# The delta-rule recurrence of a two-block network in 8 steps of 64 tokens, with one merge of the inverse from 32x32 tiles, in place of 4 chunks of 128

## The reference

```python
def step(S, inp):
    r_t, w_t, k_t, v_t, a_t, b_t = inp
    sa = jnp.einsum('bhvk,bhk->bhv', S, a_t)
    S = (S * w_t[:, :, None, :] + sa[..., None] * b_t[:, :, None, :]
         + v_t[..., None] * k_t[:, :, None, :])
    return S, jnp.einsum('bhvk,bhk->bhv', S, r_t)
...
o_rwkv = rwkv7_time_mix(rw, shift_mu, w0, w2, a0, a2, k_k, k_a, r_k,
                        ln_w, ln_b) * jax.nn.silu(rw_g)
branches = jnp.stack([o_pool, o_ret, o_rwkv], axis=2)
```

## Time and profile before

| | us |
|---|---|
| median of 3 runs | 1938.61 (1937.83 to 1939.07) |
| the profiled execution | 1933.25 |
| its span | 1931.4 |

### The profile page before, as it was taken

One profiled execution on the slowest core, in us unless ns is written; L12 is line 12 of the kernel. 1 busy time (PEld: TensorE's weight loads), 2 busy tenths in 40 slices (PEclk: granted clock), 3 DMA queues, 4 the chain that ended last, 5 costly groups with the idle time before them and its releaser, 6 DMA issues. The chain is left out here.

```text
span 1931.4 us, 24518 instructions
## 1 busy us (share of the span) xinstructions
PE 1814.2 (94%) x9920; PEld 1465.0 (76%) x9920; DVE 1107.9 (57%) x1423; ACT 775.6 (40%) x1148; POOL 645.7 (33%) x374
## 2 busy tenths in 40 slices
PE   8999999999999999899999999998999999988883
PEld 6877799888888877688988888886888987544441
DVE  5255856556777333676554766754215635967675
ACT  3346211233222344531123332234336744866673
POOL 1338411334444433661224344443441021222220
PEclk7999999999999999999999999998999999999997
DMA  8232300214555233331012355433531027999994
GB/s 330 88 110 86 100 22 1 77 56 141 186 174 185 89 120 91 105 88 56 1 55 77 120 186 176 155 121 120 167 103 43 1 90 287 378 388 395 391 395 178
DMA packets 78152, 286.44 MB, mean 148 GB/s; under 512 B 26281, under 2 KB 26409, under 8 KB 60756
## 3 DMA queue, kind: packets, MB, share of 16 engines
q1 hardware_dynamic: 72260, 274.42, 40.6%
q0 software_dynamic: 5040, 8.25, 1.3%
q10 hardware_dynamic: 736, 2.14, 0.3%
...
## 5 line engine op out<-in xcount | busy, mean ns | idle before, releaser
L1523 POOL TENSOR_TENSOR wmem_r<-wmem,wmem_r 128x1024 fp32r<-128x1024 f32 x170 | 419.2, 2467 | 652.3 <-ACT wmem_r L1035 641.3
L705 PE MATMUL banks<-h_hi_r,wmem_r 128*128 128x512 f32 x1632 | 510.4, 391 | 10.2 <-POOL wmem_r L1523 10.1
L705 PEld LDWEIGHTS banks<-h_hi_r,wmem_r 128*128 128x128 f32 x1632 | 307.0, 188 | 80.3 <-POOL wmem_r L1523 13.4
L1035 ACT ACTIVATE wmem_r<-wmem 128x1024 fp32r<-128x1024 f32 x170 | 180.1, 1060 | 438.4 <-DMA wmem<-wstream 435.2
L705 PE MATMUL banks<-hT_r,wmem_r 128*128 128x512 f32 x816 | 318.1, 390 | 0.0
L705 PEld LDWEIGHTS banks<-hT_r,wmem_r 128*128 128x128 f32 x816 | 153.6, 188 | 31.3
L2724 DVE TENSOR_TENSOR slots_r<-slots,wmem_r 128x1024 fp32r<-128x1024 f32 x102 | 122.0, 1219 | 56.2 <-ACT wmem_r L2417 50.7
L2805 POOL TENSOR_TENSOR wmem_r<-wmem,wmem_r 128x1024 fp32r<-128x1024 f32 x30 | 74.8, 2495 | 203.0 <-ACT wmem_r L2275 203.0
L1463 DVE SCALAR_TENSOR_TENSOR ztp<-xT,c_act,ztp 128x256 f32<-128x256 f32 x168 | 129.6, 771 | 6.0
L986 PE MATMUL banks<-slots_r,wmem_r 128*128 128x512 f32 x512 | 127.7, 389 | 0.0
L725 PE MATMUL banks<-wmem_r,h_hi_r 128*128 128x512 f32 x384 | 121.6, 398 | 0.0
...
...
## 6 DMA issues: line engine op xcount, KB each, us to landing
...
```

Source lines behind the costliest of these rows:

```text
L705: mm = nc.tensor.matmul(o, r(lhs[:, k, :]), r(rhs[:, k, :]), start=(k == 0 and i == 0), stop=(k == KD - 1 and i == 2))
L1035: inc(nc.scalar.activation(r(chunk(b)[0]), w, ACT.Copy), "w_high")
L1523: inc(g.tensor_tensor(r(lo), lo, r(hi), ALU.subtract), "w_split")
```

## The change

The recurrence goes in 8 steps of 64 tokens. The inverse needs one level, from 32x32 to 64x64, and that is made for all steps together before the first (`corner_products`: `zp`, then `zc`), with 32x32 matmuls. For it, the DMAs bring the inverted tiles straight into `zt`, and their transposes (a VectorE copy `inv_turned`, stored and spread too) into `tt`; ScalarE copies the off-diagonal tiles from the dg banks into the corner of `zt`.

In a step m, one half of the partitions holds the values v of its 64 tokens, the other the corrections u (`v_side`, `u_side`; they swap with m). K and b are stacked in the same way, so that one matmul over 128 rows takes both: w, s and y are each 8 matmuls of 128x64 by 64. GpSimd copies the v of even steps into `uv_even`. The state has 64 columns per pair of heads, and products with it, grams and dg take the two heads in turn, on partitions 0 to 63 and 64 to 127. The grams of step m+3 stand between w and u of step m. Masks are per step parity (`even`, `odd`) and cover keys and values at once. The LoRA products z and a alternate. GpSimd's pooling buffers move from `ztp` to `xT`.

```diff
-OFF = -DECAY * P / 2
+STEP = P // 2
+STEPS = T // STEP
+OFF = -DECAY * STEP / 2
...
+    in_step, to = row % STEP, np.arange(STEP)[None, :]
+    for name, value_rows in (("even", row < STEP), ("odd", row >= STEP)):
+        put(name, np.concatenate([in_step <= to, (in_step < to) & value_rows], 1))
...
+        uv_even = [rstd[:, :], u_sb]
+        memory = state[:, :, :].rearrange("p c f -> p (c f)")[:, 0:CW * RW_D].rearrange("p (c f) -> p c f", c=CW)
+        side_of = [slice(0, STEP), slice(STEP, P)]
+        v_side = lambda m: side_of[m % 2]
+        u_side = lambda m: side_of[(m + 1) % 2]
+        sub_of = lambda m, q: slice(u_side(m).start + q * SUB, u_side(m).start + (q + 1) * SUB)
+        uv_of = lambda m: v_tok[:, m // 2, :] if m % 2 else uv_even[m // 2 % 2]
+        bk_of = lambda m: (bk_odd if m % 2 else bk_even)[:, m // 2, :]
+        per_head = lambda a: a.rearrange("p (c e f) -> p e c f", c=CW, e=2)
...
+        GRAMS_FIRST = 3
+        for m in range(GRAMS_FIRST):
+            gram_jobs(m)
+        for name, ready in (("zp", "p_ready"), ("zc", "z_ready")):
+            for x in range(NT // 2):
+                for e in range(2):
+                    job(f"{name}{x}{e}", ready, 1 + 2 * x + e)
+        for m in range(STEPS):
+            for e in range(2):
+                job(f"w{m}{e}", "w_ready", 1 + 2 * m + e)
+            if m + GRAMS_FIRST < STEPS:
+                gram_jobs(m + GRAMS_FIRST)
+            for e in range(2):
+                job(f"u{m}{e}", "u_ready", 1 + 2 * m + e)
+            if m < STEPS - 1:
+                job(f"s{m}", "s_added", 1 + m)
+            for e in range(2):
+                job(f"y{m}{e}", "y_ready", 1 + 2 * m + e)
...
+            inc(sp.dma_start(by_row(turned_dram), inv_tmp), "inv_stored", 16)
+            after("z_clear", 1)
+            after("inv_stored", 32)
             for k in range(SUBS):
-                inc(sp.dma_start(inv_part[sub_rows(k)].rearrange("i n h j -> i (n h) j"),
-                                 inv_dram[k].rearrange("n h i j -> i (n h) j")), "inv_spread", 16)
+                q = k % 2
+                inc(sp.dma_start(zt[sub_rows(k), :, q * SUB:(q + 1) * SUB], by_sub(inv_dram, k)), "inv_spread", 16)
+                if q == 0:
+                    inc(sp.dma_start(tt[sub_rows(k), :, :], by_sub(turned_dram, k)), "inv_spread", 16)
...
-            for name, p0 in (("z", 0), ("a", 64)):
-                for c in range(CW):
+            for c in range(CW):
+                for name, p0 in (("z", 0), ("a", 64)):
...
+            for x in range(NT // 2):
+                o = [open_bank(f"dg{x}{e}") for e in range(2)]
+                for i in range(2 * CW):
+                    n, c = 2 * x + i // CW, i % CW
+                    for m in (2 * n, 2 * n + 1):
+                        for e in range(2):
+                            half = side_of[e]
+                            mm = nc.tensor.matmul(o[e][u_side(m), i * STEP:i * STEP + STEP], A_[half, c, m * STEP:m * STEP + STEP],
+                                                  KK[half, c, m * STEP:m * STEP + STEP], start=True, stop=True)
+                            if i == 2 * CW - 1 and m % 2 == 1:
+                                full(mm)
...
-                transposes(f"tb{n}", [A_[:, c, n * P:n * P + P] for c in range(CW)])
+                o = open_bank(f"tb{n}")
+                for c in range(CW):
+                    for m in (2 * n, 2 * n + 1):
+                        mm = nc.tensor.matmul(o[u_side(m), c * P:c * P + P], A_[:, c, m * STEP:m * STEP + STEP], ident, start=True, stop=True)
+                full(mm)
...
+            def gram(m):
+
+                o, t0 = [open_bank(f"gram{m}{e}") for e in range(2)], m * STEP
+                for c in range(CW):
+                    for e in range(2):
+                        half = side_of[e]
+                        for lhs, rows in ((K_, v_side(m)), (A_, u_side(m))):
+                            mm = nc.tensor.matmul(o[e][rows, c * P:c * P + P].rearrange("p (k t) -> p k t", k=2), lhs[half, c, t0:t0 + STEP],
+                                                  slots[half, 0::8, c, t0:t0 + STEP], start=True, stop=True)
+                        if c == CW - 1:
+                            full(mm)
...
+            def corner_products(name, lhs, rhs, to):
+
+                for x in range(NT // 2):
+                    if name == "zc":
+                        after("p_ready", 2 * x + 2)
+                    o = [open_bank(f"{name}{x}{e}") for e in range(2)]
+                    for i in range(2 * RW_H):
+                        for e in range(2):
+                            at = sub_of(e, 1 - to)
+                            mm = nc.tensor.matmul(o[e][sub_of(e, to), i * SUB:i * SUB + SUB], lhs(at, 2 * RW_H * x + i), rhs(at, 2 * RW_H * x + i),
+                                                  start=True, stop=True)
+                            if i == 2 * RW_H - 1:
+                                full(mm)
+
+            for m in range(GRAMS_FIRST):
+                gram(m)
+            after("inv_spread")
+            after("corner_ready")
+            corner_products("zp", lambda at, i: zt[at, i, SUB:STEP], lambda at, i: tt[at, i, :], 1)
+            corner_products("zc", lambda at, i: tt[at, i, :], lambda at, i: zt[at, i, SUB:STEP], 0)
+            after("tok_ready")
+            heads = [slice(c * RW_D, c * RW_D + RW_D) for c in range(CW)]
...
+            def state_part(o, z, m, rows, first, last):
+
+                for c in range(CW):
+                    for e in range(2):
+                        half = side_of[e]
+                        mm = nc.tensor.matmul(o[e][rows, heads[c]], z[half, c, m * STEP:m * STEP + STEP], memory[half, c, :],
+                                              start=(first and c == 0), stop=(last and c == CW - 1), skip_group_check=True)
...
+            for m in range(STEPS):
+                uv, bk = per_head(uv_of(m)), per_head(bk_of(m))
+
+                after("gram_ready", 2 * m + 2)
+                if m % 2 == 0:
+                    after("v_copied", m // 2 + 1)
+                o_w = [open_bank(f"w{m}{e}") for e in range(2)]
+                for e in range(2):
+                    for c in range(CW):
+                        mm = nc.tensor.matmul(o_w[e][u_side(m), heads[c]], gm[:, m % 4, e, c, 1, :], uv[:, e, c, :],
+                                              start=(c == 0), stop=(m == 0 and c == CW - 1), skip_group_check=True)
+                    if m == 0:
+                        full(mm)
+                if m > 0:
+                    after("s_ready", m)
+                    state_part(o_w, KK, m, u_side(m), False, True)
+                if m + GRAMS_FIRST < STEPS:
+                    gram(m + GRAMS_FIRST)
+
+                for e in range(2):
+                    o_u = open_bank(f"u{m}{e}")
+                    after("w_ready", 2 * m + e + 1)
+                    after("z_ready", 2 * (m // 4) + 2)
+                    for c in range(CW):
+                        mm = nc.tensor.matmul(o_u[u_side(m), heads[c]], zt[u_side(m), RW_H * (m // 2) + 2 * c + e, :],
+                                              w_sb[u_side(m), e * CW * RW_D + c * RW_D:e * CW * RW_D + (c + 1) * RW_D], start=True, stop=True)
                     full(mm)
-                for g in range(2):
...
+
+                if m < STEPS - 1:
+                    o_s = open_bank(f"s{m}")
+                o_y = [open_bank(f"y{m}{e}") for e in range(2)]
+                if m > 0:
+                    state_part(o_y, R_, m, v_side(m), True, False)
+                after("u_ready", 2 * m + 2)
+                if m < STEPS - 1:
                     for c in range(CW):
-                        nc.tensor.matmul(o[:, c * P:c * P + P], z[:, c, t0:t0 + P], state[:, c, :],
...
+                        for e in range(2):
+                            mm = nc.tensor.matmul(o_s[side_of[e], heads[c]], bk[:, e, c, :], uv[:, e, c, :], start=True, stop=True)
                     full(mm)
-                if n == 0:
...
+                for e in range(2):
                     for c in range(CW):
-                        cols = slice(c * P, c * P + P)
...
+                        mm = nc.tensor.matmul(o_y[e][v_side(m), heads[c]], gm[:, m % 4, e, c, 0, :], uv[:, e, c, :],
+                                              start=(m == 0 and c == 0), stop=(c == CW - 1), skip_group_check=True)
                     full(mm)
...
+            for m in range(STEPS):
+                for e in range(2):
+                    inc(nc.scalar.activation(w_sb[u_side(m), e * CW * RW_D:(e + 1) * CW * RW_D], bank(f"w{m}{e}")[u_side(m), 0:CW * RW_D], ACT.Copy), "w_ready")
+                if m % 2 == 1 and m // 2 < RING:
+                    high(FIRST["retq"] + m // 2)
+                for e in range(2):
+                    o = bank(f"y{m}{e}")[v_side(m), 0:CW * RW_D].rearrange("p (c f) -> p c f", c=CW)
```

(26 more changed lines are left out.)

319 lines of the change are left out of this document (81 added, 238 removed).

## The result

The median is 1837.47 us (four runs, 1833.72 to 1840.28) against 1938.84 for the kernel before on the same chip: a ratio of 0.9489, with an interval of 0.9476 to 0.9503, or 101 us less. The rival that says that row groups overlap (1856) was nearest.

The account below looks back on a forecast made before the run. TensorE's own work was taken to bound the recurrence. Per layer -21.4 + 1.4 + 5.4 - 1.5 - 1.9 - 1.4 = -19.4 us, -38.8 in both, from the median 1938.61: 1900 us, range 1850 to 1942.

Parts of the forecast that it names:

- The unit of 62 ns: Recurrence: each recorded fp32 matmul pass in the change's new forms costs 62 ns; 1232 passes make 76.4 us per layer.
- rival 1: Recurrence: row groups overlap, 848 alternating passes at 40 ns; -41.2 us per layer, 1856 us; chance 0.25.
- rival 2: w, y and s: full-height passes stay at 112 ns; -1.0 us per layer, 1937 us, no change; chance 0.08.
- Diagonal and turned products: Ahead of the recurrence, per layer: diagonal products 7.9 us, +1.4; turned corrections 7.2 for 1.8 us, +5.4.
- LoRA: LoRA products: z and a alternate between row groups and overlap throughout, 3.4 us and the tail; -1.5 us per layer.
- clock behind the stage: Behind the recurrence: full clock instead of half at the projection; -1.4 us per layer.
- GpSimd: TensorE's 1.95 us wait before 202.72 goes, as TensorE gets there some 5 us later; -1.9 us per layer.
- Changes of form: Recurrence steps: two changes per step between 64- and 128-row forms, 0.1 us each, 1.6 us.
- Waits in the steps: Steps 5 to 7: without a gram between w and u, u waits 0.7 us each, 2.1 us.
- way back: Recurrence steps: u1's copy (428 ns) ends under y-state products (1.0 us); 1.1 us behind s lie under y and next w.
- The inverse: Before the merges: in place near 246, TensorE comes for it at 248, so it costs nothing.
- Rival 3: Merges and steps: clock falls; whole stage at half is +49.6 us per layer, 2038 us; chance 0.12.

Follow-up runs that it names:

- a4: Kernel before with only order changed: a pair's two heads alternate in its grams, z and a in the LoRA products; 1930.08 us, ratio 0.9977.
- a3: Kernel after with the same instructions reordered so that neither row groups nor column sides alternate within a run; 1866.40 us, ratio 0.9651.

## Why the prediction was wrong

**The unit of 62 ns: the step that failed.** I took L874 (one quarter, 64 weight columns, 62 to 68 ns) and L1974 (alternating row groups, 63 ns), saw the same number, and read it as a floor on every pass. The two rows differ in two things: L1974 loads 128 weight columns. a4 shows what its alternation brings: L819's form goes from 75 to 56 ns when the groups alternate (5.03 and 3.84 us, less a tail of 0.3, over 63). So 63 was the overlapped price of a dear form, and 62 the lone price of a cheap one, and there was no floor. The right comparison was L1974 with L819, one form in two orders, 63 ns against 77; L792, which alternates at 71, made it look like little.

And the trace of before did hold the form that I said no row shows, 128 rows with 64 weight columns, and two column sides in turn, in the last block (its 16 matmuls write the two sides alternately):

```profile
1625.92 1.14 PE L2176 MATMUL banks<-ztp 128*64 128x47 f32 x32
1626.99 1.22 PE L2168 MATMUL banks<-ztp,hT 128*128 128x64 f32 x9
```

That is 33 ns a pass, what s takes in the kernel after. So "none of its short runs is faster than about 62 ns" was false, and this one row would have refuted the floor before any run.

The Trainium skill (TensorE: Matmul & The Clock Gate, Part 1, "Wait — 56ns, not 53.3ns?") states the floor that made me sure, about 62 ns per matmul where the sequencer's software decodes it; here 64 matmuls, 128 passes, take 2.10 us, 33 ns each, so that floor doesn't bind in this kernel.

**The sum.** The recurrence was forecast at 81.1 us and is 60.7 and 56.4. By the runs, the error of 62 us splits into 28 for what a lone pass costs (a3: 67 gained where 39 were forecast) and 31 for the overlap; the 3 left are within the intervals. The traces place the parts: a3's two stages take 142.8 us where 162.2 were forecast and the kernel after needs 117.0, and most of the rest of both lies in the diagonal and turned products ahead of them. The sum by rival 1 (1856, 40 ns for what alternates) had half of the mechanism: it used 40 ns where 15 to 33 were measured, and left the column sides out. That it came within 19 us is in part luck, as it also lacks the late inverse and the half clock.

**Full height.** Right: w and y take 58 to 64 ns with 64 weight columns where 128 took 112; rival 2 fell.

**Diagonal and turned products.** From the bonus products on, L810 took 2.1 us (7.9 forecast) and L821 3.9 for 64 passes (7.2). But TensorE then waits 1.34 us for ScalarE's copies of the blocks, for banks: from L810 to the rg projection it is 12.1 us, 11.8 before. The +6.8 became +0.3.

**LoRA, clock behind the stage, GpSimd.** The first two right: 1.8 us less for the LoRA products and 1.4 less from their start to the bonus products (1.5 forecast); the retention projection starts at full clock, and the stretch behind it, up to the merge of the branches, is 1.6 us shorter (1.4 forecast). The wait for GpSimd's chunk did not go: 1.95 us before, 0.8 after in layer 0, since TensorE gets there 1 us later and not 5; over the execution these waits fell from 10.1 to 6.9 us.

**Changes of form.** Right, 0.1 us each: y goes on to the next w, of the same form, after 0.93 us, and w to the state products, of another, after 1.03.

**Waits in the steps.** Right in place: w's copy in steps 5 to 7 (0.5 us each, 0.7 forecast). Not foreseen: u's copy holds s for 0.2 to 0.6 us in each step, as the y-state products over it, priced at 1.0 us, take about half. The way back that was "covered at this pace" was covered only at that pace.

**The inverse.** Its own time was about right (in place at 244.3, 246 forecast). TensorE came at 241.7, not 248, since the stage began at 238.8 and not 242.4, and the grams took 2.9 us and not 6. It was priced at nothing by a cover that depended on the failed unit; a price per us of lateness was given, but no sum with faster passes was made with it. Rival 1's sum lacks it too.

**The clock.** Rival 3 came true for 17.1 of 60.7 and 10.2 of 56.4 us, at its place (merges and step 0) and not in the steps, and not enough to decide anything.
